# Layer norms of a two-block transformer kernel: the next stage's first tile computed on the unnormed residual

## The reference

```python
def layer_norm(x, g, b):
    xf = x.astype(jnp.float32)
    mu = jnp.mean(xf, axis=-1, keepdims=True)
    var = jnp.mean(jnp.square(xf - mu), axis=-1, keepdims=True)
    return ((xf - mu) * lax.rsqrt(var + LN_EPS) * g + b).astype(x.dtype)

for i in range(DEPTH_2):                      # 2 layers
    mix = nsa_pool_mixer(x, ...) if i % 2 == 0 else gla_mixer(x, ...)
    x = layer_norm(ALPHA * x + mix, ln1_g[i], ln1_b[i])
    x = layer_norm(ALPHA * x + sqrelu_mlp(x, mlp_w1[i], mlp_w2[i]), ln2_g[i], ln2_b[i])
```

## Time and profile before

| | |
|---|---|
| median of 3 runs | 1885.6 us (1885.33 to 1886.79) |
| profiled execution | 1885.04 us, of which the span of instructions is 1883.2 us |
| busy: TensorE products, weight loads | 1860.6 us (99%), 1509.1 us (80%) |
| busy: DVE, ACT, POOL | 787.8 us (42%), 437.9 us (23%), 1080.8 us (57%) |
| granted TensorE clock | 0.999 of full speed |

### The profile page before, as it was taken

One profiled execution on the slowest core, in us unless ns is written; L12 is line 12 of the kernel. 1 busy time (PEld: TensorE's weight loads), 2 busy tenths in 40 slices (PEclk: granted clock), 3 DMA queues, 4 the chain that ended last, 5 costly groups with the idle time before them and its releaser, 6 DMA issues.

```text
span 1883.2 us, 24377 instructions
## 1 busy us (share of the span) xinstructions
PE 1860.6 (99%) x8990; PEld 1509.1 (80%) x8990; DVE 787.8 (42%) x1285; ACT 437.9 (23%) x853; POOL 1080.8 (57%) x622
## 2 busy tenths in 40 slices
PE   7999999999999999999999999999999999999998
PEld 5878887888888888876878888887877878888887
DVE  6774432353342434687551212127833561212123
ACT  5223422310010122156240101024414240101020
POOL 5755752576757657520556655565852656666652
PEclk9999999999999999999999999999999999999999
DMA  6322331232333324210223232222321233333331
GB/s 229 110 79 93 109 94 41 90 101 92 117 94 112 94 83 148 89 46 1 78 79 100 90 100 89 89 90 90 109 92 45 77 100 101 101 101 92 98 101 45
DMA packets 47455, 173.78 MB, mean 92 GB/s; under 512 B 5264, under 2 KB 5904, under 8 KB 46736
## 3 DMA queue, kind: packets, MB, share of 16 engines
q1 hardware_dynamic: 46800, 169.54, 28.3%
q10 hardware_dynamic: 576, 3.11, 0.4%
HBM read 170.53 MB, written 2.10 MB: 92 GB/s over the span
## 4 chain that ended last, share of the span: by engine, by line
PE 97%; DVE 2%; ACT 1%; DMA 0%; issue 0%; SPq 0%; DVEq 0%
PE acc L517 17%; PE acc L519 17%; PE acc L518 17%; PE acc L544 6%; PE acc L541 6%; PE acc L540 6%; PE acc L596 1%; PE acc L1013 1%; PE acc L598 1%; PE acc L597 1%; PE misc L1029 1%; PE misc L1049 1%; PE acc L1205 1%; PE acc L1207 1%; PE acc L1206 1%; PE acc L617 1%
## 5 line engine op out<-in xcount | busy, mean ns | idle before, releaser
L2674 POOL TENSOR_SCALAR w_hi<-raw 128x1024 fp32r<-128x1024 f32 x309 | 336.0, 1087 | 749.6 <-PE acc L544 277.5
L2676 POOL TENSOR_TENSOR w_lo<-raw,w_hi 128x1024 fp32r<-128x1024 f32 x309 | 749.7, 2426 | 25.8
L517 PE MATMUL acc<-x_hi,w_hi 128*128 128x512 f32 x872 | 340.1, 390 | 0.0
L519 PE MATMUL acc<-x_hi,w_lo 128*128 128x512 f32 x872 | 339.3, 389 | 0.0
L518 PE MATMUL acc<-x_lo,w_hi 128*128 128x512 f32 x872 | 339.3, 389 | 0.0
L1999 DVE TENSOR_TENSOR h<-acc,h 128x512 f32<-128x512 f32 x112 | 77.4, 691 | 357.1 <-PE acc L519 226.4
L519 PE MATMUL acc<-y_hi,w_lo 128*128 128x512 f32 x540 | 210.1, 389 | 0.0
L518 PE MATMUL acc<-y_lo,w_hi 128*128 128x512 f32 x540 | 210.1, 389 | 0.0
L517 PE MATMUL acc<-y_hi,w_hi 128*128 128x512 f32 x540 | 210.1, 389 | 0.0
L519 PEld LDWEIGHTS acc<-x_hi,w_lo 128*128 128x128 f32 x872 | 163.7, 188 | 34.0
L517 PEld LDWEIGHTS acc<-x_hi,w_hi 128*128 128x128 f32 x872 | 163.7, 188 | 34.0 <-issue 0.3
(11 more groups left out here) (491 smaller groups left out, 2799.9 us busy)
## 6 DMA issues: line engine op xcount, KB each, us to landing
raw<-weights_dram SPq DMA_DIRECT2D x309, 512.0 KB, 3.5
h<-x_dram SPq DMA_DIRECT2D x2, 1024.0 KB, 6.0
out_dram<-out_tok SPq DMA_DIRECT2D x6, 256.0 KB, 2.1
small<-small_dram SPq DMA_DIRECT2D x1, 1408.0 KB, 15.7
mem_in<-mem_dram SPq DMA_DIRECT2D x1, 1024.0 KB, 12.8
w_cmp<-w_cmp_dram ACTq DMA_DIRECT2D x1, 1024.0 KB, 7.1
small<-small_dram ACTq DMA_DIRECT2D x1, 992.0 KB, 4.9
const<-const_dram SPq DMA_DIRECT2D x1, 640.0 KB, 8.9
```

The source lines that it names most:

```text
L517: mm(out, m["w_hi"][:, slot, k], hi[:, k], start=k == 0, stop=False)
L519: last = mm(out, m["w_lo"][:, slot, k], hi[:, k], start=False, stop=k == kc - 1)
L2674: nc.gpsimd.tensor_scalar(hi, m["raw"][:, slot], 1.0, 0.0, ALU.mult, ALU.add).then_inc(sem("weights_high"), 1)
L2676: nc.gpsimd.tensor_tensor(m["w_lo"][:, slot].rearrange("p k n -> p (k n)"), m["raw"][:, slot], bf(hi), ALU.subtract).then_inc(sem("weights ...
```

## The change

- TensorE computes the first tile of the stage behind each of the three norms on the residual before its norm, times the gain (`plain_opening`). The residual's sum, centre and scale are put in when the tile leaves: output = rstd x (W(g h) - mean x Wg) + Wb. The three tiles that are worked on together are then the second to the fourth.
- For this ACT writes a high part of gain x h for each chunk (`plain_high`), and DVE the low part (`plain_low`): chunk 0 behind the sixth addition, chunk 1 ahead of the eighth and last, the others behind it.
- TensorE multiplies the tile's weights by four columns, high and low parts of gain and bias (`plain_columns`, 16 products with 4 columns each). ACT and DVE take the result out.
- DVE puts mean and scale in (`plain_fix`) ahead of the third normed chunk, ACT adds the bias and writes the tile back to its PSUM bank behind the last normed chunk.
- The four products of L678 behind each of the three norms go. The third bank of scaled chunks is now that of the first tile, not the fourth. ACT writes a copy of the mean.
- The first round of each mlp stage stands ahead of the loop in TensorE's program. Some semaphores are merged.

```diff
+    def plain_opening(norm):
+        i, first = LAYER_NORMS.index(norm), START[BEFORE_STAGE[norm]]
+        slot = first % RING
+        claim(first)
+        for k in range(KC):
+            pe.wait_ge(sem("plain_ready"), (KC + 1) * i + k + 2)
+            mm(acc[:, slot], m["w_hi"][:, slot, k], x_hi[:, k], start=k == 0, stop=False)
+            mm(acc[:, slot], m["w_hi"][:, slot, k], x_lo[:, k], start=False, stop=False)
+            last = mm(acc[:, slot], m["w_lo"][:, slot, k], x_hi[:, k], start=False, stop=k == KC - 1)
+            last.then_inc(sem("plain_read" if k < KC - 1 else "tile_done"), 1)
+        pe.wait_ge(sem("plain_cols_out"), i + 1)
+        opening(first + 1, first + 1, norm)
+
+    def plain_columns(norm):
+        ...
+        pe.wait_ge(sem("weights_split"), first + 1)
+        pe.wait_ge(sem("tile_out"), first - 2)
+        pe.wait_ge(sem("plain_ready"), (KC + 1) * i + 1)
+        for k in range(KC):
+            mm(out, m["w_hi"][:, slot, k], m["gb_r"][:, k], start=k == 0, stop=False)
+            last = mm(out, m["w_lo"][:, slot, k], m["gb_r"][:, k], start=False, stop=k == KC - 1)
+        last.then_inc(sem("plain_cols"), 1)
...
+        plain_columns(name)
         pe.wait_ge(sem("tile_out"), first)
         mm(misc[:, 0, :], ones, m["h"][:, KC - 1], start=False, stop=True).then_inc(sem("ln_mean"), 1)
         pe.wait_ge(sem("norm_sq"), chunks_before(name) + KC)
         mm(summed, ones, m["sq"][:, (KC - 1) % 2], start=False, stop=True).then_inc(sem("norm_summed"), 1)
-        idle_products(4, first % RING)
...
+        def plain_high(k):
+            f(m["x_hi"][:, k], m["h"][:, k], ACT.Copy, scale=pr.col(gain, at + k)).then_inc(sem("plain_high"), 1)
+
         for k in range(HALF):
             act.wait_ge(sem("ln_centred"), HALF * i + k + 1)
             square(name, k, m["h"])
+            plain_high(k)
...
             act.wait_ge(sem("tile_out"), t0 + k + 1)
             square(name, k, m["h"])
+            plain_high(k)
+        act.wait_ge(sem("plain_cols"), i + 1)
+        f(m["gb_cols"], acc[:, (first + 1) % RING, 0:4], ACT.Copy).then_inc(sem("plain_cols_out"), 1)
         act.wait_ge(sem("ln_mean"), 2 * i + 2)
         f(m["sq"][:, 0], misc[:, 0, :], ACT.Square, scale=1.0 / D).then_inc(sem("ln_mean_sq"), 1)
+        f(m["mean"], misc[:, 0, :], ACT.Copy).then_inc(sem("ln_mean_sq"), 1)
...
         high_chunks(name, high, keep)
+        act.wait_ge(sem("plain_fixed"), i + 1)
+        act.wait_ge(sem("norm_kept"), KC * (KEPT.index(name) + 1))
+        own.link(f(acc[:, first % RING], z[:, first % RING], ACT.Identity, bias=m["gb_sum"][:, 1:2]))
...
+        own.mark(v.tensor_scalar(m["gb_f"], pr.view(gain)[:, at:at + KC], -1.0 / D, None, ALU.mult))
+        own.mark(v.tensor_copy(gb[:, :, 1], bias))
+        own.settle()
+        own.mark(v.tensor_copy(gb[:, :, 0], m["gb_f"]))
+        own.mark(v.tensor_tensor(gb[:, :, 3], bias, bf(gb[:, :, 1]), ALU.subtract))
+        own.settle()
+        v.tensor_tensor(gb[:, :, 2], m["gb_f"], bf(gb[:, :, 0]), ALU.subtract).then_inc(sem("plain_ready"), 1)
+
+        def plain_low(k):
+            dve.wait_ge(sem("plain_high"), KC * i + k + 1)
+            v.scalar_tensor_tensor(m["x_lo"][:, k], h[:, k], pr.col(gain, at + k), bf(m["x_hi"][:, k]),
+                                   ALU.mult, ALU.subtract).then_inc(sem("plain_ready"), 1)
+
+        def plain_fix():
+            slot = first % RING
+            dve.wait_ge(sem("tile_done"), first + 1)
+            own.settle()
+            own.link(v.scalar_tensor_tensor(z[:, slot], m["mean"], m["gb_sum"][:, 0:1], acc[:, slot], ALU.mult, ALU.add))
+            v.tensor_tensor(z[:, slot], z[:, slot], rstd, ALU.mult).then_inc(sem("plain_fixed"), 1)
...
             if k < KC - 1:
                 add_squares(name, k)
+            if k == KC - 3:
+                plain_low(0)
             if k == KC - 2:
                 for x, (whole, parts) in enumerate(((part, "sum_hl"), (rstd, "sq_hl"))):
                     dve.wait_ge(sem("ln_high"), SUMS_LATE + 3 * i + x + 2)
                     v.tensor_tensor(m[parts][:, 1], whole, bf(m[parts][:, 0]), ALU.subtract).then_inc(sem("ln_low"), 1)
+                plain_low(1)
         dve.sem_inc(sem("norm_added"), 1)
...
+        plain_low(2)
+        plain_low(3)
+        dve.wait_ge(sem("plain_cols_out"), i + 1)
+        own.mark(v.tensor_tensor(m["gb_sum"], m["gb_cols"][:, 0:2], m["gb_cols"][:, 2:4], ALU.add))
         dve.wait_ge(sem("norm_summed"), NORMS.index(name) + 1)
...
+        plain_low(4)
+        dve.wait_ge(sem("ln_mean_sq"), 2 * i + 2)
         centred = [centre(k) for k in range(2)]
+        plain_low(5)
+        plain_low(6)
 
         def scale(k):
+            if k == 2:
+                plain_fix()
             own.settle(centred[k])
...
+            if k == 0:
+                plain_low(KC - 1)
```

More of the change, by code:

```diff
@@ L341, in memory_map @@
     place("ones_r", [P], F32R, region(4 * P))
+    place("gb_r", [KC, 4], F32R, region(4 * 4 * KC))
+    place("gb_f", [KC], F32, region(4 * KC))
+    place("gb_cols", [4], F32, region(16))
+    place("gb_sum", [2], F32, region(8))
     small = region(4 * max(columns(SMALL1)[1], columns(SMALL2)[1]))
@@ L423, in norm_banks @@
             return self.misc[:, 0, MEM:2 * MEM], self.misc[:, 0, 0:n], [self.misc[:, b, 0:n] for b in (3, 1, 2)]
-        fourth = (START[BEFORE_STAGE[name]] + 3) % RING
+        fourth = (START[BEFORE_STAGE[name]] + (0 if name in LAYER_NORMS else 3)) % RING
         return self.misc[:, 2], self.misc[:, 1], [self.misc[:, 3], self.misc[:, 1], self.acc[:, fourth]]
@@ L523, in dense @@
                 after(k)
+    def plain_opening(norm):
[11 more added lines that the diff above has]
+    def plain_columns(norm):
+        i, first = LAYER_NORMS.index(norm), START[BEFORE_STAGE[norm]]
+        slot = first % RING
+        out = acc[:, (first + 1) % RING, 0:4]
+        pe.wait_ge(sem("weights_split"), first + 1)
[5 more added lines that the diff above has]
+        last.then_inc(sem("plain_cols"), 1)
     def opening(t0, first_tile, norm):
@@ L634, in stage @@
             late_opening(START[name], START[name], norm)
-        elif norm:
-            opening(START[name], START[name], norm)
-        for i in range(3 if norm else 0, n):
+        elif norm in LAYER_NORMS:
+            plain_opening(norm)
+        for i in range(4 if norm in LAYER_NORMS else 3 if norm else 0, n):
             t = START[name] + at + i
@@ L959, in tensor_program @@
     pe.wait_ge(sem("tile_out"), t0 + 1)
-    pe.wait_ge(sem("r_col"), 1)
+    pe.wait_ge(sem("gate_parts"), 2)
     for tb in range(TB):
@@ L1117, in mlp_group @@
         t0 = g * 16 + START[name]
-        opening(t0, START[name], norm)
-        for j in range(3, 8):
+        plain = isinstance(g, int) and g == 0
+        if plain:
+            plain_opening(norm)
+        else:
+            opening(t0, START[name], norm)
+        for j in range(4 if plain else 3, 8):
             dense(t0 + j, (START[name] + j) % RING, x_hi, x_lo)
@@ L1129, in mlp @@
     def mlp(name, norm, high, next_norm=None):
-        with pe.Fori(0, GROUPS - 1) as g:
+        mlp_group(name, 0, norm, high)
+        with pe.Fori(1, GROUPS - 1) as g:
             mlp_group(name, g, norm, high)
@@ L1390, in residual_rms @@
                 slot = START["nsa_in"] % RING
-                f(m["w_hi"][:, slot, :, 32:56], bf(m["w_lo"][:, slot, :, 0:24]), ACT.Copy).then_inc(sem("gates_stacked"), 1)
+                f(m["w_hi"][:, slot, :, 32:56], bf(m["w_lo"][:, slot, :, 0:24]), ACT.Copy).then_inc(sem("gate_parts"), 1)
             if k >= 2:
@@ L1408, in residual_ln @@
         f(m["sum_hl"][:, 0], m["sum_h"], ACT.Copy).then_inc(sem("ln_high"), 1)
+        gain, at = name[:3] + "_g", KC * (name[3] == "b")
+        first = START[BEFORE_STAGE[name]]
+        def plain_high(k):
+            f(m["x_hi"][:, k], m["h"][:, k], ACT.Copy, scale=pr.col(gain, at + k)).then_inc(sem("plain_high"), 1)
         for k in range(HALF):
@@ L1621, in scalar_program @@
     act.wait_ge(sem("r_turned"), 1)
-    f(m["r_col"], misc[:, 3, 0:TB], ACT.Copy).then_inc(sem("r_col"), 1)
+    f(m["r_col"], misc[:, 3, 0:TB], ACT.Copy).then_inc(sem("gate_parts"), 1)
     act.wait_ge(sem("gates_turned"), 1)
-    f(m["gate_t"], misc[:, 3, 256:512].rearrange("p (b n) -> p b n", b=TB)[:, :, 0:24], ACT.Copy).then_inc(sem("gate_high"), 1)
+    f(m["gate_t"], misc[:, 3, 256:512].rearrange("p (b n) -> p b n", b=TB)[:, :, 0:24], ACT.Copy).then_inc(sem("gate_parts"), 1)
     act.wait_ge(sem("cmp_zeroed"), 1)
@@ L1932, in residual_ln @@
         rstd, summed, banks = pr.norm_banks(name)
+        gain, at = name[:3] + "_g", KC * (name[3] == "b")
+        first = START[BEFORE_STAGE[name]]
+        gb, bias = m["gb_r"], pr.view(name[:3] + "_b")[:, at:at + KC]
+        own.mark(v.tensor_scalar(m["gb_f"], pr.view(gain)[:, at:at + KC], -1.0 / D, None, ALU.mult))
[10 more added lines that the diff above has]
+        def plain_fix():
```

(5 more changed lines are left out.)

13 lines of the change are left out of this document (8 added, 5 removed).

## The result

The changed kernel takes **1907.1 us** (median of 4 runs, 1906.43 to 1908.2) beside 1886.2 us of the kernel before (1885.33 to 1886.91, 4 runs on the same chip): ratio **1.0112, 95% interval 1.0101 to 1.0124**. The forecast was 1893.1 us, between 1884.5 and 1899. The sign was right; the loss is 21 us and not 7.5.

The account below looks back on a forecast made before the run. TensorE, busy 99% of the span, was taken as the bound. Three norms at 2.43 us plus 0.2 at `gla_in` made 7.5 us on 1885.04: 1892.5, or 1893.1 us by the median; range 1884.5 to 1899.

Parts of the forecast that it names:

- the mechanism and its times: At each norm, DVE's low parts of chunks 0 and 1 wait for POOL's subtractions; last addition 4.05 us late.
- 0.4 us of safety: The low part of chunk 0 starts behind POOL's subtraction's start, and stays so unless ACT is 0.4 us faster.
- the size of a norm at full clock: Each of the three norms costs 2.4 to 2.5 us more than before, three 7.3 us.
- the blocking ahead of the last addition: DVE's low parts held up by POOL at each norm: 1.8 us of the stalls there.
- The rival without blocking: Low parts slip past POOL's subtractions, DVE is full all the same: 0.6 us a norm, 1887.7 us; chance 0.20.
- a rival of its own: TensorE's clock falls at each norm once the empty products go: 8 us more, 1901 us; chance 0.08.
- the four empty products: Unread TensorE products at each norm; removing them and the wait behind them takes away 3.79 us a norm.
- the `gla_in` stage at 0.2 us: The gate's input is ready slightly late for TensorE: 0.2 us, between nothing and 3 us.
- the columns: 16 four-column products at each norm, 1.7 us, mostly covered by TensorE's wait for the last addition; cost 0.1 us.
- DVE's six small operations: Preparation for the columns ahead of the first addition, where DVE idles: nothing; without that cover some 1 us.
- the first mlp round put ahead of the loop: Peeling the loop's first round leaves TensorE's stream as it was: nothing.
- the plain tile fills TensorE: From the sums to the opening's end nothing stalls much: 2.6 us saved a norm, 1877.9 us; chance 0.10.

Follow-up runs that it names:

- e7: Kernel before with one more DVE operation at each norm, both operands in SBUF, result unread, where the low part of chunk 0 goes; 1885.4 us (one execution).
- e9: Changed kernel with the low part of chunk 0 one place earlier, ahead of the addition of the sixth chunk's squares; 1895.2 us.
- e10: Changed kernel whose operation for the low part of chunk 0 stays in place but reads the half sums in PSUM, not the chunk in SBUF; 1893.0 us.
- e1: Changed kernel with two empty float32 products put in TensorE's wait at each norm, ahead of the product of the split sums; 1898.8 us.
- e12: e9 with one empty product a norm and early write back of the first tile, without that tile's low parts on DVE (TensorE's work the same); 1885.9 us.
- e2: Changed kernel with the low parts of chunks 0 and 1 moved behind the last addition; 1895.7 us.
- e5: e2 with one empty product added in TensorE's wait at each norm; 1895.7 us.
- e3: Kernel before with the four empty products behind each norm's sums left out and nothing in their place; 1891.4 us.
- e14: Changed kernel with one empty product in TensorE's wait for `sum_hl` at each norm; 1902.1 us.

## Why the prediction was right or wrong

- **Right: the mechanism and its times.** The low part of chunk 0 took 2.87 us, the one of chunk 1 1.80, and the last addition came at the time worked out. The Trainium skill ("SBUF — State Buffer", Who interferes with whom) says that the one that issues first keeps the shared port and the other is blocked. The traces agree: DVE was 0.07 us behind in the kernel after and waited, and 0.10 us ahead in e7, where POOL waited. The prediction said 0.4 us of safety, and there was less. It also left out that POOL's shorter step, the high part, holds such an operation up too (e9, e10).
- **Right: the size of a norm at full clock.** Forecast 2.43 us a norm, 7.3 for three. e1, where the clock holds, has 9.4, of which 1.9 is a wait that is named below: 7.5. Of these, the blocking ahead of the last addition is (9.38 - 4.17) / 3 = 1.7 us a norm (e1 against e9; forecast 1.8). The rival without blocking was put at 0.6 us a norm; e9 has 4.17 - 1.84 = 2.3 for three, 0.8 each.
- **Wrong, the step that failed: the sum put the clock at nothing and kept it as a rival of its own.** The prediction counted the four empty products as 3.79 us removed, and held the clock's fall unlikely (0.08) since the clock was 0.999 in a kernel with short waits. But the waits at the norms were the ones that these products filled. The fall doesn't compete with blocking either: blocking makes the idle time at L697 that lowers the clock. Both came true, 6.5 us at the norms. The size that the rival gave, up to 8 us, was about right; the sum with it would have been some 1900 us, so this step is the largest miss and not the whole of it.
- **Wrong: the `gla_in` stage at 0.2 us.** The gate product itself had no wait worth naming, as forecast (0.3 us from opening to gate). The cost was 30 us further on: 1.8 us of wait for `k_g`, and in the profiled execution of the kernel after 1.6 us more, as the clock fell behind this wait too (in e1 and e12, with the same wait, it held). The prediction asked when the gate's input was ready and not where POOL would be in its splitting by then.
- **Missing: the first tile's bank.** ACT writes the tile back as its last act (972.47), and the tile behind the opening waits for that bank and for `y_lo`: 0.51 and 1.35 us. The prediction listed this write back at the gate alone.
- **Not foreseeable: 1.6 us between 127 and 130 us**, in code ahead of the change, where the clock fell to 0.50 in the profiled executions of after, e2 and e5 and in none of the others. Why there is open, and that the change causes it isn't shown.
- **Nothing, as forecast:** the columns (1.7 us at full clock, 16 products at 0.11 us), DVE's six small operations, the first mlp round put ahead of the loop.

The sum with what was measured: 7.5 (norms at full clock) + 1.9 (`y_lo`) + 6.5 (clock at the norms) + 3.6 (`gla_in`) + 1.8 (ahead of the norms) = 21.3, against 21.7. It is an account of two executions: the part of the clock changes from one to the next.

The rival "the plain tile fills TensorE" (-2.6 us a norm) had its point in DVE's low parts: without them (e12) a norm gives 0.5 to 1.25 us. So the idea is sound on TensorE, and what it costs on DVE, eight low parts with both operands in SBUF, is more than it brings. Even in e9 the first four took 0.99 + 1.21 + 2.67 = 4.9 us, where two take 1.4 with POOL idle.

## What to carry to other kernels

Work that nobody reads, standing in a wait, can be free and hold TensorE's clock; before it goes, ask how long TensorE then idles, and count the clock into the sum together with the wait that causes it, not as another case. Where a DVE operation with two SBUF operands meets POOL, look at the distance between their starts: a tenth of a microsecond decided which of them was held up (DVE by 2.2 us, or POOL by 0.5), and one place in the program order won most of it back. When a stage's last step moves against POOL's stream of splits, follow POOL to its next pause, not only to the next product.

## What was new of the hardware

- Idling of 2.0 us with the split sums and four-column products behind it lowered the granted clock to 0.50 at each of three norms, for 6.8, 3.4 and 6.8 us of a busy TensorE; idling of 3.6 us alone did so too (e3). With 1.12 us of idling (e14) it fell at two norms of three. Four-column products without a wait ahead left it at 1.00 (e2), while other small products at 127 us went with a fall in three profiled executions of 16.
- DVE (two SBUF operands) and POOL hold each other up in both directions, decided by starts 0.07 to 0.10 us apart: DVE 2.87 us in place of 0.7, or POOL 2.91 in place of 2.41. POOL's step with a single SBUF operand holds DVE up as well (0.99 us, e9).
- Products of four columns with full 128x128 weights come every 0.11 us, as those with 64 columns did. The Trainium skill ("TensorE: Matmul & The Clock Gate", Back-to-back issue gap) has 25 ns as the floor of a small product; these lie four times above it. Each brings a weight load of its own; that the loads set the pace is not shown.
